# Gate matmuls in half pieces between the recurrence levels, a weight split moved behind the first decays, and five search rounds moved into the heads

## What is computed

```python
(q, k, v, iq, ik, iw, hq, hf, hi, hg, ga, gb) = jnp.split(h @ w_in, IN_OFFSETS, axis=-1)
...
attn = attend(q, k, v, iq, ik, iw, pos).reshape(B, T, WIDTH_A)
zf = hf.astype(jnp.float32)
logf = jnp.log(lb + (1.0 - lb) * jax.nn.sigmoid(zf))
kf = (1.0 - lb) * jax.nn.sigmoid(-zf)
o, s_new = hgrn2_chunked(jax.nn.silu(hq)..., kf..., logf..., hi..., s0)
o = rms_norm(o.astype(h.dtype), o_norm) * jax.nn.silu(hg...)
merged = jax.nn.sigmoid(ga) * (attn @ w_proj_attn) + jax.nn.sigmoid(gb) * (o.reshape(B, T, WIDTH_B) @ w_proj_hgrn)
return merged @ w_out, k, v, ik, s_new
```

## Time and profile before

| what | us |
|---|---|
| median of 3 runs | 1739.26 |
| lowest and highest run | 1734.11, 1740.22 |
| the profiled execution, own time | 1732.57 |
| its span, first to last instruction | 1730.5 |
| mean granted TensorE clock | 0.982 of full |

### The profile page before, as it was taken

The page is one execution under the profiler, slowest core; times in us unless marked ns, Lnnn a source line. Parts: engine busy times, 40 slices in busy tenths (PEclk is TensorE's granted clock), DMA queues, the critical chain, the costliest instruction groups (busy, mean ns, idle before and its releaser), DMA issues.

```text
span 1730.5 us, 29178 instructions
## 1 busy us (share of the span) xinstructions
PE 1646.1 (95%) x12749; PEld 1512.9 (87%) x12753; DVE 732.0 (42%) x1190; ACT 445.7 (26%) x629; POOL 697.0 (40%) x584
## 2 busy tenths in 40 slices
PE   7999999999998899967999999998999999999998
PEld 6999999999957899956888765657999999999998
DVE  6323012334316589478574644435643222022311
ACT  4112111212452224300233333332233111111211
POOL 4333444446321245655144342341443434443432
PEclk9999999999999999988899999999999999999999
DMA  6222233423411223201522277998223222322222
GB/s 180 74 73 76 84 104 98 116 76 108 159 30 40 66 98 90 81 27 51 174 77 80 77 268 274 422 411 331 74 74 91 80 66 84 103 78 74 83 68 89
DMA packets 193502, 203.59 MB, mean 118 GB/s; under 512 B 6224, under 2 KB 179344, under 8 KB 184928
## 3 DMA queue, kind: packets, MB, share of 16 engines
q1 hardware_dynamic: 173040, 105.56, 21.3%
q0 software_dynamic: 12832, 80.29, 12.3%
q10 hardware_dynamic: 7504, 15.88, 2.4%
HBM read 187.21 MB, written 14.30 MB: 116 GB/s over the span
## 4 chain that ended last, share of the span: by engine, by line
PE 89%; DVE 4%; ACT 2%; DMA 2%; issue 1%; POOL 1%; ACTq 0%; SPq 0%; DVEq 0%; POOLq 0%
PE ps L1596 25%; PE ps L1597 24%; PE ps L1598 24%; PE ps L2048 3%; PE ps L2065 1%; PE ps L2123 1%; PE ps L1994 1%; DMA k_page<-in_cache_k,kv_row 1%; PE ps L2012 1%; PE ps L2003 1%; PE ps L1926 1%; DVE k_lev L1302 1%; DVE n_lo L1024 1%; PE ps L1609 1%; DVE att L1282 1%
## 5 line engine op out<-in xcount | busy, mean ns | idle before, releaser
L489 POOL TENSOR_TENSOR w_lo<-raw,w_hi 128x512 fp32r<-128x512 f32 (+1 forms) x398 | 525.9, 1351 | 784.1 <-ACT w_hi L642 784.1
L1596 PE MATMUL ps<-n_lo,w_hi 128*128 128x288 f32 x1824 | 544.0, 298 | 1.0 <-ACT qT L748 1.0
L1597 PE MATMUL ps<-n_hi,w_lo 128*128 128x288 f32 x1824 | 538.6, 295 | 0.0
L1598 PE MATMUL ps<-n_hi,w_hi 128*128 128x288 f32 x1824 | 536.8, 294 | 0.0
L1596 PEld LDWEIGHTS ps<-n_lo,w_hi 128*128 128x128 f32 x1824 | 342.4, 188 | 15.5 <-issue 14.4
L1598 PEld LDWEIGHTS ps<-n_hi,w_hi 128*128 128x128 f32 x1824 | 344.0, 189 | 0.0
L1597 PEld LDWEIGHTS ps<-n_hi,w_lo 128*128 128x128 f32 x1824 | 343.0, 188 | 0.1
L642 ACT ACTIVATE w_hi<-raw 128x2048 fp32r<-128x2048 f32 (+2 forms) x108 | 188.0, 1740 | 268.5 <-PE ps L1598 268.4
L1597 PE MATMUL ps<-hid_hi,w_lo 128*128 128x288 f32 x704 | 208.4, 296 | 0.0
L1596 PE MATMUL ps<-hid_lo,w_hi 128*128 128x288 f32 x704 | 208.4, 296 | 0.0
L1598 PE MATMUL ps<-hid_hi,w_hi 128*128 128x288 f32 x704 | 208.1, 296 | 0.0
(11 more groups left out here) (302 smaller groups left out, 2278.2 us busy)
## 6 DMA issues: line engine op xcount, KB each, us to landing
raw<-in_ffn_w_gate SPq DMA_DIRECT2D x44, 512.0 KB, 3.9
raw<-in_ffn_w_up SPq DMA_DIRECT2D x44, 512.0 KB, 5.2
raw<-in_ffn_w_down SPq DMA_DIRECT2D x32, 704.0 KB, 4.7
raw<-in_w_in SPq DMA_DIRECT2D x22, 1024.0 KB, 5.3
gates<-scratch_g ACTq DMA_DIRECT2D x4, 1152.0 KB, 9.8
raw<-in_w_out SPq DMA_DIRECT2D x4, 1024.0 KB, 5.1
scratch_g<-g_ring POOLq DMA_DIRECT2D x7, 576.0 KB, 3.1
scratch_x<-xT ACTq DMA_DIRECT2D x1, 2304.0 KB, 11.9
```

The source lines that it names most:

```text
L489: ins = pool.tensor_tensor(w_lo[:, u % NRAW, part], raw[:, u % NRAW, part], w_hi[:, u % NW, part].bitcast(F32), ALU.subtract)
L1596: pe.matmul(dst, hi, x_lo, start=first, stop=False)
L1597: pe.matmul(dst, lo, x_hi, start=False, stop=False)
L1598: return pe.matmul(dst, hi, x_hi, start=False, stop=last)
```

## The change

Sixteen half pieces (the 8 pieces of gate units 0 and 1, 12 matmuls each) stand in `heads(0)` and `heads(1)`, one after each level, in banks 0 to 3; ACT copies them into a small ring `g_head`, SP stores them unscaled, and POOL scales their quarter after it was read back for the projections. The prompt attention keeps 24 pieces: two ahead, whole ones in steps 0 to 13, half pieces in steps 14 to 29. Gate unit 1's low half moves from ahead of `decays(0)` to behind it; those of units 2 and 3 follow `decays(1)` and the state stores. Five of the 16 search rounds leave steps 11 to 15 and stand in `heads(0)` ahead of the first masked merge. The other edits rename semaphores and adapt counts.

```diff
+def gate_quarter(n):
+
+    return (n // 2 + 3) % 4
...
-    for g in range(DC // 2):
-        w_in("gate", 2 * g, OGA + 256 * g, 256)
-        w_in("gate", 2 * g + 1, OGB + 256 * g, 256)
+    for n in range(DC):
+        q = gate_quarter(n)
+        w_in("gate", n, (OGB if n % 2 else OGA) + 256 * q, 256)
...
+        PRE, FULL = 2, 14
+
+        def piece_of_step(n):
+
+            return (2 * HB + PRE + n, (0, 1)) if n < FULL else (2 * HB + PRE + FULL + (n - FULL) // 2, ((n - FULL) % 2,))
+
+        PIECES = 4 * HA
+
+        def g_piece(i):
+
+            n, at = i // 4, i % 4 * HT
+            return g_head[:, i % 3, :] if i < 2 * HB else g_out(n)[:, at:at + HT]
+
+        def g_home(n):
+
+            return scratch_g[2 * gate_quarter(n) + n % 2]
+
         def g_out(n):
...
+            def store_piece(i):
+                sp.wait_ge(S("gate_out"), i + 1)
+                at = i % 4 * HT
+                sp.dma_start(g_home(i // 4)[:, at:at + HT], g_piece(i)).then_inc(S(f"head_stored{i % 3}"), 16)
+
             for u in range(NRAW, U):
+                n = u - NRAW - at_unit["gate", 0]
+                if n in (0, 1):
+                    for i in range(4 * n, 4 * n + 3):
+                        store_piece(i)
                 load_unit(u)
+                if n in (0, 1):
+                    store_piece(4 * n + 3)
 
...
-                for n in range(8):
+                for n in range(2, 8):
...
                     ins.then_inc(S("gate_scaled"), 1)
-                    pool.wait_ge(S("gate_scaled"), n + 1)
-                    pool.dma_start(scratch_g[n], g_out(n)).then_inc(S(f"gate_stored{n % 2}"), 16)
+                    pool.wait_ge(S("gate_scaled"), n - 1)
...
+                pool.wait_ge(S("quarter_in3"), X_IN[3] + 16)
+                at = GATES_AT[3]
+                for n in range(2):
+                    for a in range(2):
+                        part = gates[:, at + n, a, :]
+                        ins = pool.tensor_tensor(part, part, rms[:, :], ALU.mult)
+                ins.then_inc(S("gate_scaled"), 1)
...
-            lows(at_unit["feat", 5] + 2)
+            lows(at_unit["gate", 0])
...
                 decays(g)
+                lows(at_unit["gate", g + 1])
                 state_store(2 * g)
                 state_store(2 * g + 1)
+            lows(at_unit["gate", 3])
...
-                n, at = i // 4, i % 4 * HT
-                if i % 4 == 0:
-                    split(at_unit["gate", n] + 1)
+                n = i // 4
                 if i % 4 == 3:
                     act.wait_ge(S("unit_done"), at_unit["gate", n] + 1)
                 else:
                     act.wait_ge(S("gate_half"), 3 * n + i % 4 + 1)
-                if 2 <= n < 7:
-                    act.wait_ge(S(f"gate_stored{n % 2}"), 16 * (n // 2))
-                act.activation(g_out(n)[:, at:at + HT], ps[:, 6 + i % 2, 0:HT], ACT.Copy).then_inc(S("gate_out"), 1)
+                if 3 <= i < 2 * HB:
+                    act.wait_ge(S(f"head_stored{i % 3}"), 16 * (i // 3))
+                elif 4 <= n < 7:
+                    act.wait_ge(S(f"gate_stored{n % 2}"), 16 * ((n - 2) // 2))
+                bank = i % 4 if i < 2 * HB else 6 + i % 2
+                act.activation(g_piece(i), ps[:, bank, 0:HT], ACT.Copy).then_inc(S("gate_out"), 1)
+                if i % 4 == 3:
+                    split(at_unit["gate", n] + 2)
 
             def heads(g):
+                for i in range(4 * g, 4 * g + 4):
+                    gate_out(i)
                 for a in range(2):
...
-                    if n + 1 < 4 * HA:
-                        gate_out(n + 1)
+                    if n == 0:
+                        gate_out(2 * HB + 1)
+                    elif piece_of_step(n - 1)[1][-1] == 1 and piece_of_step(n - 1)[0] < PIECES:
+                        gate_out(piece_of_step(n - 1)[0])
...
+                    if g == 3:
+                        act.wait_ge(S("gate_scaled"), 7)
...
+                if g == 3:
+                    for m in range(3):
+                        act.wait_ge(S(f"head_stored{m}"), 16 * len(range(m, 2 * HB, 3)))
...
+            EARLY = 5
...
+                        if h == 0 and L == 1:
+                            take(EARLY)
                         level_out(a, L - 1)
...
-                    if n < 16:
+                    if n < 16 - EARLY:
                         take(1)
...
-            def gate_half(i):
+            def gate_piece(i, part):
 
                 n, a, t = i // 4, i // 2 % 2, i % 2
                 hi, lo = unit(at_unit["gate", n])
-                if i >= 2:
-                    pe.wait_ge(S("gate_out"), i - 1)
-                for k in range(DC):
+                head = i < 2 * HB
+                if part[0] == 0 and i >= 4:
+                    pe.wait_ge(S("gate_out"), i - 3 if head else i - 1)
+                bank = i % 4 if head else 6 + t
+                for k in range(DC // 2 * part[0], DC // 2 * part[-1] + DC // 2):
                     at = k * 256 + a * P
-                    ins = product(ps[:, 6 + t, 0:HT], hi[:, at:at + P], lo[:, at:at + P],
+                    ins = product(ps[:, bank, 0:HT], hi[:, at:at + P], lo[:, at:at + P],
                                   n_hi[:, k, t * HT:(t + 1) * HT], n_lo[:, k, t * HT:(t + 1) * HT],
                                   k == 0, k == DC - 1)
-                ins.then_inc(S("unit_done" if i % 4 == 3 else "gate_half"), 1)
+                if part[-1] == 1:
+                    ins.then_inc(S("unit_done" if i % 4 == 3 else "gate_half"), 1)
 
             def heads(g):
...
+                    gate_piece(4 * g + L // 2, (L % 2,))
...
+                    pe.wait_ge(S("gate_out"), 4 * g + 4)
...
-                gate_half(0)
+                gate_piece(2 * HB, (0, 1))
...
-                    if n + 2 < 4 * HA:
-                        gate_half(n + 2)
+                    if piece_of_step(n)[0] < PIECES:
+                        gate_piece(*piece_of_step(n))
...
```

More of the change, by code:

```diff
@@ L272, in build @@
         state_s, e = sb("state_s", [P, 2, NB, VD], at=e)
+        g_head, e = sb("g_head", [P, 3, HT], at=e)
+        assert e <= mix_at + 75008
         v_own, e = sb("v_own", [NS, 2, NB, VD], at=bias_at - 4 * (256 + 384 + 512))
@@ L437, in build @@
         SMALL_IN = 16 * 8
+        X_IN = (32, 16, 16, 16)
         SCORE_AT = {2: 0, 3: 256, 4: 640}
@@ L525, in attention_pages @@
                 value_group(6)
[L526 removed]
+                for n in range(2, 8):
                     lows(min(at_unit["gate", n] + 2, at_unit["proj", 0]))
                     if n == 6:
[L529 removed]
+                        pool.wait_ge(S("gate_stored1"), 32)
                         value_group(5)
                     if n == 7:
[L532 removed]
+                        pool.wait_ge(S("gate_stored0"), 48)
                         value_group(4)
@@ L873, in turned @@
                                    .rearrange("p (s q) -> p s q", s=t), ACT.Copy).then_inc(S("ppT_done"), 1)
-                gate_out(0)
+                gate_out(2 * HB)
                 for n in range(4 * HA):
@@ L898, in prompt_attention @@
                 turned(4 * HA - 1)
-                split(at_unit["gate", 7] + 2)
             def sample_attention():
@@ L926, in turned @@
                         if j == 0 and pair == 0:
-                            act.wait_ge(S("gate_stored1"), 64)
+                            act.wait_ge(S("gate_stored1"), 48)
                         if j < 4:
@@ L1573, in _ @@
             features(0)
-            while taken[0] < 2 * ROUNDS - 4 * HA:
+            while taken[0] < 2 * (ROUNDS - 16):
                 take_half()
@@ L1603, in x_in @@
                     if c % 2 == 0:
-                        pe.wait_ge(S(f"x_in{c // 2}"), 16 if c else 32)
+                        pe.wait_ge(S(f"quarter_in{c // 2}"), X_IN[c // 2])
                     if c >= 4:
@@ L2022, in prompt_attention @@
                 pe.wait_ge(S("state_s_done"), HB)
-                gate_half(1)
+                gate_piece(2 * HB + 1, (0, 1))
                 pe.wait_ge(S("v_back"), 16)
```

13 lines of the change are left out of this document (6 added, 7 removed).

## The result

The changed kernel takes **1727.5 us** (median of four runs, 1723.4 to 1730.5), the kernel before 1739.7 beside it. The ratio is 0.9929, 95% interval 0.990 to 0.9957: 12.3 us faster (7.5 to 17.4) where 26.3 were forecast. The time lies half a microsecond above the range of 1703 to 1727. The profiled execution had 1723.37 us, span 1721.4.

The account below looks back on a forecast made before the run. DVE was taken to bound the levels of both heads, PE the prompt attention. Terms -5.0, +2.9, +4.0, -5.0 and -23.2 sum to -26.3 us, from the median 1739.26 to 1713.0 us; range 1703 to 1727.

Parts of the forecast that it names:

- start of heads(0): Heads(0) up to the last operands: decays start 6.06 us earlier, levels cost +1.1; -5.0 us.
- POOL beside DVE: Last operands and `v_own` in both heads: POOL's moved low halves lengthen DVE's two-input operations; +2.0 us each, +4.0 together.
- tail of heads(0): Behind the levels of heads(0): no term in the sum, 0 us.
- levels of heads(1): Levels of heads(1): PE becomes the bound with the half pieces, and no gap stands ahead; +2.9 us.
- tail of heads(1): Window 821 to 843: the clock recovers from 0.66 because PE is busy in the levels; -5.0 us, bounds 0 and -7.5.
- sample attention: Stage behind the prompt attention: starts earlier as a block, its length counted as unchanged, 0 us.
- the attention term: Prompt attention, steps 14 to 29: half pieces save 26.2 us of PE work, stalls cost 3.0; -23.2 us.
- The stall: Step 24 of the prompt attention: DVE does more than the shortened step lasts; 1.4 us.
- The meeting with POOL: Prompt attention, some shortened step: a DVE instruction becomes long beside POOL's; up to 1.75 us, counted as 1.2.
- the search rounds: Heads(0) ahead of the first merge: 13.0 us of rounds hidden in DVE's 17.32 us of idle time; cost 0.
- the gates' late scaling: Projections: POOL scales the last gates for 5.6 us until 1205.3, hidden with 3 us to spare.
- Rival (e): Tail of heads(1) stays at the low clock: 1718 us; 0.83 jointly with the forecast and one other rival.

Follow-up runs that it names:

- after: The first profile of the changed kernel itself; median 1727.5 us, ratio 0.9929 against the kernel before, profile span 1721.4 us.
- again: The changed kernel once more, unaltered; 1723.2 us, ratio 0.9922.
- quiet_split: On top of `quiet`, the sample biases of step 24 are made in two steps, 24 and 25; 1704.6 us, ratio 0.983.
- quiet: The changed kernel with POOL's low halves of gate units 1 to 3 moved behind the fourth state of the first head of each heads; 1711.0 us, ratio 0.985.
- before_again: The kernel before once more, unaltered; profile span 1735.2 us.
- after_spread: The changed kernel with only the sample's small products spread through the state steps; 1728.6 us, ratio 0.995.
- quiet_early0: On top of `quiet`, the five search rounds are back in steps 11 to 15 of the prompt attention; 1709.1 us, ratio 0.9853.
- quiet_split2: The kernel `quiet_split` once more, unaltered, on another chip; 1707.3 us, ratio 0.9818.
- low1_back: The changed kernel with the low half of gate unit 1 made ahead of the first decays again; 1723.4 us, ratio 0.993.
- thin_heads: On top of `quiet`, half of the matmuls of the 16 half pieces in the levels left out; profile span 1706.0 us.
- bare_heads: On top of `quiet`, all but 3 of the 12 matmuls of each half piece in the levels left out; profile span 1712.0 us.
- spread_small: On top of `quiet_split`, the sample's 8 small products per head spread through its four state steps; 1701.4 us, ratio 0.9788.
- reorder: On top of `spread_small`, DVE takes each head's `state_s` behind that head's states and POOL makes one low half in each heads; 1697.1 us, ratio 0.9768.
- no_small: On top of `quiet`, 6 of the 8 matmuls of the sample output per head left out; profile span 1695.9 us.

## Why the prediction was half right

The stages give the sum again, mean of `after` and `again` less mean of the two profiles of before; for S, which scatters, the median of the fourteen profiles with the change takes the place of that mean (with it, S would be +4.2 and the sum -11.6):

| step of the sum | forecast | measured |
|---|---|---|
| start of heads(0), its levels (A) | -5.0 | -5.6 |
| POOL beside DVE (B and E) | +4.0 | +6.2 |
| tail of heads(0) (C) | 0 | +3.4 |
| levels of heads(1) (D) | +2.9 | +1.4 |
| tail of heads(1) (F) | -5.0 | +0.5 |
| prompt attention (G) | -23.2 | -21.7 |
| sample attention (S) | 0 | +1.3 |
| sum | -26.3 | -14.5 |

The sum agrees with both ratios (12.3 and 13.5 us) within their intervals. 11.8 us are missing. Two steps of the prediction failed: the clock in the tails (-5.0 counted for heads(1) and nothing for heads(0), measured +0.5 and +3.4) and, smaller, the term for POOL beside DVE.

- **Right:** the attention term. A plain shortened step is 1.57 to 1.6 us shorter (5.66 to 4.06, 6.23 to 4.66), nearly the 1.64 of a half piece. The stall stood in step 24, as said, and was 1.9 us where 1.4 was counted. The meeting with POOL that I had put down for some step (1.2 us) is this very one, and what I had read as DVE's own load of the step was mostly POOL (before, the two biases took 3.15 us beside its subtraction; in `quiet_split`, 0.61 each); new is that the clock fell behind it and took 1.5 us more in step 25.
- **Right:** the start of heads(0). DVE's wait for the decays is down from 7.63 us to 1.53, its wait before the first merge from 17.32 to 4.52, the values that the prediction named.
- **Right:** the search rounds are free, and the gates' late scaling is hidden, as POOL's timeline shows where the earlier trace rows had 23.72 us of idle time:

```profile
1186.55 5.56 POOL L601 TENSOR_TENSOR gates<-gates,rms 128x576 f32<-128x576 f32 x4 [15.17 <-DMA gates<-scratch_g]
1200.16 6.32 POOL L525 TENSOR_TENSOR w_lo<-raw,w_hi 128x512 fp32r<-128x512 f32 x4 [8.05 <-ACT w_hi L687]
```

- **Right in kind, too dear:** the levels of heads(1). PE became their bound and cost +1.4 us.
- **Mis-sized: POOL beside DVE.** The bounds were 0 and 4 a stage, and I took the middle; it is 3.1. The exposed operations take 3.87 us against 2.33 (both v_own), 1.21 against 0.74 and 1.82 against 0.74, which is the 3.1. I also priced only units 1 and 2. Unit 3's low half was moved in front of the attention pages too, beside the output gating: 5.5 us of DVE time more (8.50 against 3.0). Little of it shows: dots(0) starts at 851.90, before the gating is done, the step from dots(1) to dots(2) takes 4.15 and 4.01 us (`after`, `again`) against 3.94 before, and S is 177.7 in `again` and 177.6 in `quiet`.
- **Wrong: the clock.** The prediction read the fall in the tail of heads(1) as the result of a level phase with PE busy for two thirds, and so gave 5.0 us back. The levels are now busy throughout at clock 1.00, and the tail's is 0.66 all the same. Rival (e) had named this outcome, at 1718, without a cause. Part of the reading stands: before, the fall came already at the first waits of the tail (`before_again`, the same product at 0.98 and 1.25 us), and with the levels filled and POOL quiet a like wait leaves the clock up (0.71 in `quiet`).

```profile
820.42 0.98 PE L1934 MATMUL ps<-cst,k_lev 128*64 128x128 f32 x5 [1.27 <-DVE att L1282]
...
822.36 1.25 PE L1934 MATMUL ps<-cst,k_lev 128*64 128x128 f32 x5 [0.97 <-DVE att L1282]
```

But the tail holds two more things that go ahead of a fall: the wait that POOL's overlap lengthened to 2.76 us (enough by itself, `after_spread`), and the string of small products. With the levels filled and POOL quiet, F is still 24.0 us in three profiles of four; with the string spread it is 16.7. The change brought the long wait into both tails, and the tail of heads(0), at full clock before, fell as well. There the wait isn't the whole account: with 1.20 us in its place C is 16.6 to 18.5 (`quiet`, `quiet_early0`, `quiet_split`, `quiet_split2`, `low1_back`) against 14.9 before, so about half of the +3.4, or more, is open. The two terms for the tails miss 8.9 us.

The two misses hang together in part. `quiet` takes away POOL's overlap alone and gets 12.1 us. In the profiles 6.2 of them are B and E, and those are DVE's longer operations themselves; 1.8 are in C, 1.9 in F (24.0 against a mean of 26.0), less 0.7 in D; the rest of the 12.1 isn't placed. The profile of `quiet` is also 1.6 us shorter in G, nearly all in step 25, but three kernels with POOL in the same place (`quiet_early0`, `thin_heads`, `bare_heads`) have G at 140.9 like the changed kernel: that part doesn't come from POOL's place. So a term that I had bounded by 4 us a stage, for the instructions themselves, carried slower tails with it, 3.7 us in these profiles; the share of C isn't firm, since `low1_back` and `quiet_split` have 18.2 and 18.5 without the long wait.

The prediction had the rule for it beside the sum. The Trainium skill (GPSIMD Engine Reference, section Specifications) says that GpSimd's SBUF interfaces are shared with VectorE, with contention for VectorE's instructions in a two-port mode or with two SBUF inputs. This trace agrees where two inputs are concerned: such operations become 1.6 to 2.5 times as long, and one gating stands still for 6.31 us. The search's MAX8, with one input, takes 1.22 us at 870.90 beside POOL's subtraction, as elsewhere. But one input alone doesn't protect an operation: `TENSOR_SCALAR` stood still too (3.6 us against 0.61). Whether it ran in a two-port mode, no run here shows.

## What to carry to other kernels

- When work is moved on one engine, list what the other engines do beside it in its new place: a wait on a semaphore that marks "DVE now waits for PE" put POOL's 5 us where they cost little, and was worth as much as the whole change.
- Give a wait in front of small products the price of the slow clock behind it, not only its own length, and look for a fall's cause in the tail itself as well as in the mean of the stage ahead.
- Take the length of a DMA-fed stage from more than one profile before a loss is put there.

## What the runs showed of the hardware

- A DVE instruction can stand still until POOL's have ended. With one input: 128x512 in 3.6 us against 0.61, and 64x8 in 3.16 us against 0.17, each beside a POOL multiplication of 2.8 us for two. With more inputs: one output gating, 128x576, in 6.31 us against 0.81, through four POOL subtractions in a row that started 0.7 us after it.
- POOL is slowed in some meetings and not in others: its four subtractions take 4.93 us with DVE idle (`quiet`, from 772.69), 5.02 us beside that output gating, and 7.50 us beside DVE's operands.
- In `after` and `again` the clock fell within 4 us of PE's wait of 2.7 us for DVE, in both heads; behind one of 1.2 us, in `quiet` and in heads(0) of `low1_back`, the state products ran at full speed; in heads(1) of the kernel before, whose levels left PE idle for a third, a fall stood behind 1.27 us. In step 24 a wait of 1.8 us was followed by either.
- 16 small matmuls (128x8) in a row, 1.95 us, stood ahead of 17 slow gauges of 24 where the wait was 1.2 us. The same, four at a time between 128-wide ones, or only four of them, stood ahead of none of 12 (`spread_small`, `reorder`, `no_small`).
